# An MLA and pooling step on one core: opening, query preparation, ends of attention and small weights of the merge rearranged

## The chip, the cores and the metric
The kernel runs on one core of a Trainium2 chip. It is written engine by engine: PE (matrix products and transposes), DVE (vector), ACT (activations), POOL (GpSimd) and SP (which only issues DMAs) each have their own instruction stream, and semaphores order them. The metric is the device time of one execution in microseconds. Of three runs of the kernel before the median is 2271.24 us (2266.74 to 2272.23).

## The reference
One layer of a decoder on 2048 prompt tokens and 8 sample tokens, each of the latter with 2048 positions of paged cache. Everything is float32; in the kernel every product operand is split into a high part (rounded to the type fp32r) and a low part, the rest, and a product is made as three products (high x high, high x low, low x high).
```
h = rmsnorm(x, g_pre); z = h @ w_in       # q_lat 256, kv_lat 128, k_r 64, z_att, u_pool, z_pool, g_att, g_pool
q = (rmsnorm(q_lat, g_q) @ w_uq)          # 8 heads of 128 + 64
q_r = rope(q[128:]); q_abs = einsum(q[:128], w_uk)      # 128 a head
ckv = rmsnorm(kv_lat, g_kv); kr = rope(k_r)
s = (q_abs . ckv + q_r . kr) * SCALE, causal; o_lat = softmax(s) @ ckv
y_att = (einsum(o_lat, w_uv) * silu(z_att)) @ w_o_att
p = causal window means of u_pool (2, 4, 8, 16) - u_pool, @ w_pool, * pool_scale
y_pool = (p * silu(z_pool)) @ w_o_pool
x = x + (sigmoid(g_att) * y_att + sigmoid(g_pool) * y_pool) @ w_out;  y = rmsnorm(x, g_final)
```

## The kernel before
The work is in four stages, each a block of its own in which all engines start together: `project`, `attend`, `decode` (the sample tokens' attention) and `merge`.

`project` (names a_) takes 17 tiles of 128 rows. `steps` runs them as a pipeline: step i makes h of tile i, the latent product of tile i-1, and the queries of tile i-2 and i-3. Steps 0 to 2 are written out, the rest is a loop, and steps NT to NT+2 drain it. Two hooks stand in the written-out steps: `columns` makes the high and low part of the latent weights `wlat` (ACT L295, DVE L81 in `split`), `prepare` those of the query weights `wq`. The absorbed weights w_uq x w_uk are made by PE (L445) in PSUM; DVE multiplies them and the rotary columns with g_q (L372, L375), casts (L377) and splits. PE's latent product waits for weights_ok. SP stores h, queries, ckv and krope; the block waits for all stores at its end.

`attend` (names b_; q is read back from HBM) has 32 units, 16 query tiles x 2 groups of 4 heads. Unit u belongs to query tile u // 2, and has u // 2 + 1 key tiles. Its steps are, by kind: Q the high part of the queries (ACT L728, L729; the low part is POOL's split), S scores, five products (PE L828), C copy out of PSUM with the row maximum (DVE L778, L782), B the bias (L789), E exp (ACT L735), I the inverse of the sum, P the scaling (DVE L806), T four transposes (PE L838), H and L the high part (ACT L742) and low part (DVE L81) of the transposed weights, V three products (PE L847), O the output. The queries of a unit are five DMAs on SP (L675, L679) into one of two buffers. `attend_orders` fixes the order on PE, ACT and DVE ahead of time: a planner goes through queues of steps, by estimated durations (`takes`) and by what each step needs (`needs`). The order of the queues is the order of preference; on PE it is V, T, S. DVE's work for the sample tokens' queries (e_rows, e_q, e_qd, L757 to L763) stands ahead of its first C.

`merge` (names d_) has 5 chunks of 412 columns. ORDER lists 52 products with a weight tile each (U the pooling input, ZP, ZA, GA, GP, OA, OP, WO); their weights come through two pairs of buffers, high part on ACT (L919), low part on DVE (L81), two tiles ahead. Before the first chunk the small weights w_uv and w_pool are loaded on ACT's queue into memory that zs and u use later, and split by ACT (L1456, L1457) and DVE; DVE also makes hsum, sums of the history. POOL makes the window sums (L1579 and following), and the low part of the latent outputs, ols.


## Time and profile before
| | us |
|---|---|
| median of 3 runs | 2271.24 |
| the profiled execution | 2264.78 |
| its span, first to last instruction | 2263.0 |
| PE busy | 2150.1 (95%) |
| DVE busy | 1284.1 (57%) |
| ACT busy | 990.7 (44%) |
| POOL busy | 358.1 (16%) |
| mean granted TensorE clock | 0.984 |

The busy times are sums over the whole span, and PE is busy in nearly all of it. What PE does not fill, 113 us, is at particular places, which the timeline shows: there each row gives, in brackets, how long the engine was idle before it and which instruction released it. The idle time of the other engines costs nothing in itself. The projection goes to about 248 us, attention to 940, decode to 1006, the merge to the end.

### The profile page before, as it was taken

The page shows a single profiled execution, that of the slowest core. Times are in us where ns is not written, and L with a number is a line of the kernel's source. Part 1 is how long each engine was busy: PE and PEld are TensorE (multiplying, and loading weights), DVE is VectorE, ACT ScalarE, POOL GpSimd, SP SyncE. Part 2 cuts the span into 40 slices and gives each one's busy share as a digit, 9 for nine tenths or more (in the row PEclk, how much of TensorE's full clock was granted, in tenths as well). Part 3 has the DMA queues.
Part 4 walks back from the last instruction along what each step waited for, and adds up shares of the span by engine and source line. Part 5 has one row for each costly group of instructions (what it writes and reads, how often), then busy time and mean ns, then how long its engine had stood idle before and what let it go on. Part 6 is the DMA issues. An engine that isn't in the chain of part 4 may idle for free.

```text
span 2263.0 us, 33247 instructions
## 1 busy us (share of the span) xinstructions
PE 2150.1 (95%) x11994; PEld 1988.9 (88%) x11994; DVE 1284.1 (57%) x2632; ACT 990.7 (44%) x1774; POOL 358.1 (16%) x496
## 2 busy tenths in 40 slices
PE   4999689999999999788999999999999999999997
PEld 4888578888888888568999999999999999999997
DVE  4565377778777777335544464346544464446434
ACT  3555365555555555344333443244333433334333
POOL 1333221201100020105000420015000510032000
PEclk9999799999999999899999999999999999999999
DMA  4454332211100111244443345334534345333432
GB/s 165 152 169 152 116 89 59 53 30 33 38 24 20 29 55 63 109 140 133 149 152 121 131 135 179 117 137 130 178 119 142 114 138 171 115 122 127 175 121 69
DMA packets 132142, 252.84 MB, mean 112 GB/s; under 512 B 18394, under 2 KB 82274, under 8 KB 130710
## 3 DMA queue, kind: packets, MB, share of 16 engines
q1 hardware_dynamic: 108734, 218.17, 29.8%
q10 hardware_dynamic: 20960, 20.19, 3.1%
q0 software_dynamic: 2304, 12.58, 1.4%
q8 instruction: 88, 1.44, 0.3%
q14 instruction: 56, 0.46, 0.1%
HBM read 208.34 MB, written 42.79 MB: 111 GB/s over the span
## 4 chain that ended last, share of the span: by engine, by line
PE 52%; DVE 1%; issue 1%; ACT 0%; DVEq 0%; POOLq 0%; POOL 0%; ACTq 0%
PE d_ps L113 52%; PE d_ps L1731 1%; DVE d_gate_p L1678 0%; DVE d_mrg L81 0%; DVE d_y L1635 0%; ACT d_zs L1523 0%; ACT d_mrg L1501 0%; DVE d_ya L1682 0%; ACT d_zs L1537 0%; DVE d_y L1637 0%; DVE d_pool L81 0%; DVE d_y L1716 0%; DVE d_wr L81 0%; ACT d_wr L919 0%; POOLq L1279 0%
## 5 line engine op out<-in xcount | busy, mean ns | idle before, releaser
L113 PE MATMUL d_ps<-d_ht,d_wr 128*128 128x412 f32 x3840 | 738.3, 351 | 9.7 <-DVE d_wr L81 8.0
L113 PEld LDWEIGHTS d_ps<-d_ht,d_wr 128*128 128x128 f32 x3840 | 719.1, 188 | 14.1 <-DVE d_wr L81 8.3
L81 DVE TENSOR_TENSOR d_wr<-d_ws,d_wr 128x1024 fp32r<-128x1024 f32 x260 | 320.6, 1233 | 554.7 <-ACT d_wr L919 554.5
L919 ACT ACTIVATE d_wr<-d_ws 128x1024 fp32r<-128x1024 f32 x260 | 275.2, 1059 | 603.7 <-PE d_ps L113 601.1
L828 PE MATMUL b_ps<-kt,b_qs 128*128 128x512 f32 (+3 forms) x1600 | 359.0, 376 | 18.7 <-POOL b_qs L81 14.4
L828 PEld LDWEIGHTS b_ps<-kt,b_qs 128*128 128x128 f32 x1600 | 277.4, 194 | 65.7 <-POOL b_qs L81 15.0
L735 ACT ACTIVATE b_p<-b_p,b_bias 128x1024 f32<-128x1024 f32 (+7 forms) x192 | 172.0, 898 | 109.7 <-DVE b_low L789 106.3
L81 DVE TENSOR_TENSOR b_pt<-b_ps,b_pt 128x512 fp32r<-128x512 f32 x272 | 171.9, 683 | 81.2 <-ACT b_pt L742 80.8
L847 PE MATMUL b_ps<-b_pt,kv 128*128 128x512 f32 x816 | 209.3, 399 | 8.8 <-DVE b_pt L81 8.8
L742 ACT ACTIVATE b_pt<-b_ps 128x512 fp32r<-128x512 f32 x272 | 143.7, 596 | 143.8 <-PE b_ps L838 143.3
L847 PEld LDWEIGHTS b_ps<-b_pt,kv 128*128 128x128 f32 x816 | 151.7, 189 | 47.8 <-DVE b_pt L81 14.0
L113 PE MATMUL d_ps<-d_mrg,d_wr 128*128 128x412 f32 x960 | 190.1, 353 | 0.5
L113 PE MATMUL d_ps<-d_gat,d_wr 128*128 128x412 f32 x960 | 186.6, 350 | 0.0
L113 PEld LDWEIGHTS d_ps<-d_gat,d_wr 128*128 128x128 f32 x960 | 179.3, 188 | 0.8
L113 PEld LDWEIGHTS d_ps<-d_mrg,d_wr 128*128 128x128 f32 x960 | 176.3, 188 | 4.0 <-DVE d_mrg L81 2.2
L81 POOL TENSOR_TENSOR b_qs<-b_qf,b_qs 128x512 fp32r<-128x512 f32 x64 | 86.4, 1351 | 515.8 <-ACT b_qs L729 513.3
L782 DVE TENSOR_SCALAR_CACHE_REDUCE b_p<-b_ps 128x512 f32<-128x512 f32 x192 | 130.6, 686 | 35.7 <-PE b_ps L828 27.6
L838 PEld LDWEIGHTS b_ps<-ident,b_p 128*128 128x128 f32 x1088 | 126.0, 142 | 26.1 <-DVE b_p L806 13.8
L838 PE MATMUL b_ps<-ident,b_p 128*128 128x128 f32 x1088 | 137.6, 275 | 11.7 <-DVE b_p L806 11.5
L1579 POOL TENSOR_TENSOR d_win<-d_u 128x426 f32<-128x426 f32 x20 | 21.2, 1060 | 735.8 <-ACT d_u L1482 733.2
L806 DVE TENSOR_SCALAR b_p<-b_p,b_inverse 128x1024 f32<-128x1024 f32 (+7 forms) x192 | 124.0, 676 | 1.4
L113 PE MATMUL a_ps<-a_wlat,a_ht 128*128 128x448 f32 x408 | 89.3, 375 | 6.5 <-DVE a_wlat L81 6.5
(193 smaller groups left out, 2132.5 us busy)
## 6 DMA issues: line engine op xcount, KB each, us to landing
d_ws<-in_w SPq DMA_DIRECT2D x260, 512.0 KB, 3.5
out_q<-a_qout SPq DMA_DIRECT2D x17, 768.0 KB, 3.3
a_x<-in_x ACTq DMA_DIRECT2D x17, 512.0 KB, 3.7
out_ht<-a_hf SPq DMA_DIRECT2D x17, 512.0 KB, 4.1
d_hf<-out_ht SPq DMA_DIRECT2D x20, 412.0 KB, 3.6
d_olf<-out_olat SPq DMA_DIRECT2D x40, 206.0 KB, 3.0
b_qf<-out_q SPq DMA_DIRECT2D x32, 256.0 KB, 2.8
b_qf<-out_q SPq DMA_DIRECT2D x128, 64.0 KB, 2.6
```

The source lines that it names most:

```text
L81: return e.tensor_tensor(low, source, high.bitcast(f32), ALU.subtract)
L113: mm = pe.matmul(out, stationary(a, k), moving(b, k), start=first and k == 0 and a + b == 0, stop=last and k == depth - 1 and a == 1)
L735: act.activation(sp_[row][:, keys], sp_[row][:, keys], ACT.Exp, bias=bias[:, row:row + 1], scale=SCALE, accum_out=total[:, row, part:part ...
L742: act.activation(pt[n % NPT][:, 0, :], ps_t[n % NTB][:, :], ACT.Copy).then_inc(pt_hi, 1)
L782: dve.tensor_scalar(out, inp, 1.0, None, ALU.mult, ALU.max, accum_out=top[:, row, c:c + 1]).then_inc(s_sb, 1)
L806: dve.tensor_scalar(sp_[row][:, keys], sp_[row][:, keys], inverse[:, row:row + 1], None, ALU.mult).then_inc(p_ok, 1)
L828: mm = pe.matmul(ps_s[n % NS][:, 0:keys * P], q[:, a, h, :], kt[:, first:first + keys, b, :], start=k == 0, stop=k == len(pairs) - 1)
L838: mm = pe.transpose(ps_t[n % NTB][:, h * P:h * P + P], sp_[(u % 2) * HG + h][:, j * P:j * P + P], ident[:, :])
L847: mm = pe.matmul(ps_o[u % 2][:, :], kv[:, j, a, :], pt[n % NPT][:, b, :], start=j == 0 and k == 0, stop=j == tiles(u) - 1 and k == 2)
L919: act.activation(ahead["wr"][k % 2][:, 0, :, :], ahead["ws"][k % 4][:, :, :], ACT.Copy).then_inc(ahead["w_hi"], 1)
L1579: own(pool.tensor_tensor(out[:, start:HIST + T], source[:, start:HIST + T], source[:, start - shift:HIST + T - shift], ALU.add))
L1731: mm = pe.transpose(bank[xt_bank(n)][0:rows, s * P:s * P + P], yt[n % 2][:, s * P:s * P + rows], ident[:, :])
```

## The change
In the projection, g_pre, the small weights and all other inputs are loaded on SP, wlat in two halves with a semaphore each; ACT loads no inputs, and loads its table with a one-column activation at its start. It no longer waits for g_pre and the identity before its first square. PE starts the first latent product with the first half of the inner dimension. g_q is applied to the query latent of every tile (a scale in ACT's copies, a scalar_tensor_tensor on DVE) instead of to the weights. On ACT the first instructions were

```order
L287 DMA a_wuq_t<-in_w_uq_t 128x2048
L288 DMA a_wuk_t<-in_w_uk_t 128x1024
L289 DMA a_wq_f<-in_w_uq_rope 128x2x512
L302 ACT_TABLE_LOAD
L302 ACTIVATE a_junk,a_stat<-a_x 128x1024
L307 DMA a_x<-in_x 128x1024
L336 ACTIVATE a_hf<-a_ps 128x512 x2
L295 ACTIVATE a_wlat<-a_wlat_f 128x1792 x2
```

and are

```order
L314 ACT_TABLE_LOAD
L314 ACTIVATE a_warm<-a_half 128x1
L343 ACTIVATE a_junk,a_stat<-a_x 128x1024
L348 DMA a_x<-in_x 128x1024
L379 ACTIVATE a_hf<-a_ps 128x512 x2
L320 ACTIVATE a_wlat<-a_wlat_f 128x1792 x2
L343 ACTIVATE a_junk,a_stat<-a_x 128x1024
L348 DMA a_x<-in_x 128x1024
```

The three input loads are gone from ACT's queue, and a table load with `a_warm` stands first.

The buffers of attention's queries and their semaphores now belong to both stages; wlat_f and wuk_t lie in their memory during the projection. SP loads units 0 and 1 (k_qf_49 and k_qf_50, stores a_qout) before the last two stores of queries, in SP's rows of the projection's end:

```order
L243 DMA out_ht<-a_hf 1024x1x128
L249 DMA out_q<-a_qout 128x1536
L254 DMA out_ckv<-a_norm 128x128
L257 DMA out_krope<-a_norm 128x64
L550 DMA k_qf_49<-out_q 128x512
L554 DMA k_qf_49<-out_q 64x2x128 x4
L550 DMA k_qf_50<-out_q 128x512
L554 DMA k_qf_50<-out_q 64x2x128 x4
L249 DMA out_q<-a_qout 128x1536 x2
```

Before, no L550 or L554 stood there, and the stores followed each other. ACT and POOL make the high and low parts of these queries at the projection's end. The block does not wait for the stores; SP, ACT, POOL and DVE do so at the start of `attend`, PE does not.

In attention, the first eight units (SMALL) have their scores in memory of their own, so that C does not wait for an earlier unit's transposes. PE's preferences are T, V, S, and the last unit's scores go first once they are reached. `takes` has other durations and there are lags behind Q. The decode queries' work on DVE stands before unit 16's first C. PE began (b_qs the queries, kt the keys, b_p the weights of the softmax, b_pt these transposed)

```order
L828 MATMUL b_ps<-kt,b_qs 128x128 x40
L828 MATMUL b_ps<-kt,b_qs 128x256 x15
L838 MATMUL b_ps<-ident,b_p 128x128 x8
L828 MATMUL b_ps<-kt,b_qs 128x256 x10
L847 MATMUL b_ps<-b_pt,kv 128x512 x6
L828 MATMUL b_ps<-kt,b_qs 128x256 x15
L828 MATMUL b_ps<-kt,b_qs 128x384 x15
L838 MATMUL b_ps<-ident,b_p 128x128 x12
L828 MATMUL b_ps<-kt,b_qs 128x384 x5
L847 MATMUL b_ps<-b_pt,kv 128x512 x9
```

and begins (k_qs_51 and k_qs_52 are the two buffers of the queries)

```order
L911 MATMUL b_ps<-kt,k_qs_51 128x128 x20
L911 MATMUL b_ps<-kt,k_qs_52 128x128 x20
L911 MATMUL b_ps<-kt,k_qs_51 128x256 x20
L911 MATMUL b_ps<-kt,k_qs_52 128x256 x20
L911 MATMUL b_ps<-kt,k_qs_51 128x384 x20
L911 MATMUL b_ps<-kt,k_qs_52 128x384 x20
L911 MATMUL b_ps<-kt,k_qs_51 128x512 x20
L911 MATMUL b_ps<-kt,k_qs_52 128x512 x20
L911 MATMUL b_ps<-kt,k_qs_51 128x512 x5
L911 MATMUL b_ps<-kt,k_qs_51 128x128 x5
L911 MATMUL b_ps<-kt,k_qs_51 128x512 x5
L921 MATMUL b_ps<-ident,b_p 128x128 x4
```

The transposes (L921) and products (L930) of the first units stand behind the scores of units 0 to 8. At attention's end PE did

```order
L828 MATMUL b_ps<-kt,b_qs 128x512 x5
L847 MATMUL b_ps<-b_pt,kv 128x512 x3
L838 MATMUL b_ps<-ident,b_p 128x128 x12
L847 MATMUL b_ps<-b_pt,kv 128x512 x9
L838 MATMUL b_ps<-ident,b_p 128x128 x12
L847 MATMUL b_ps<-b_pt,kv 128x512 x9
L838 MATMUL b_ps<-ident,b_p 128x128 x12
L847 MATMUL b_ps<-b_pt,kv 128x512 x9
```

and does

```order
L911 MATMUL b_ps<-kt,k_qs_51 128x384 x5
L911 MATMUL b_ps<-kt,k_qs_52 128x512 x15
L921 MATMUL b_ps<-ident,b_p 128x128 x16
L930 MATMUL b_ps<-b_pt,kv 128x512 x3
L921 MATMUL b_ps<-ident,b_p 128x128 x8
L930 MATMUL b_ps<-b_pt,kv 128x512 x3
L921 MATMUL b_ps<-ident,b_p 128x128 x4
L930 MATMUL b_ps<-b_pt,kv 128x512 x3
L921 MATMUL b_ps<-ident,b_p 128x128 x4
```

Each tile's transposes are followed by another tile's products, and the last unit's scores stand before them.

In the merge, w_pool, w_uv and the history have memory of their own (inside mrg's), are loaded by SP behind two weight tiles, and their splitting stands behind step 1 of the first chunk. PE waits for it only before the first ZP product. Waits on const_in, y_zero and small_ok at the start of ACT are gone (y_zero is waited for before the first square), and the waits `wait_all(..., const_in, ...)` on all engines are `after(...)`, without const_in. ACT's rows at the start of the merge were

```order
L1453 DMA d_u<-in_w_pool 128x4x128
L1454 DMA d_zs<-in_w_uv 128x4x256
L1456 ACTIVATE d_wuv<-d_zs 128x1024
L1457 ACTIVATE d_wpl<-d_u 128x512
L919 ACTIVATE d_wr_9960<-d_ws_10884 128x1024
L1482 ACTIVATE d_u<-d_ps 128x412
L919 ACTIVATE d_wr_9961<-d_ws_10885 128x1024
L1482 ACTIVATE d_u<-d_ps 128x412
```

and are

```order
L1002 ACTIVATE d_wr_9945<-d_ws_10869 128x1024
L1569 ACTIVATE d_u<-d_ps 128x412
L1002 ACTIVATE d_wr_9946<-d_ws_10870 128x1024
L1543 ACTIVATE d_wuv<-d_wuv_f 128x1024
L1544 ACTIVATE d_wpl<-d_wpl_f 128x512
L1569 ACTIVATE d_u<-d_ps 128x412
L1621 ACTIVATE d_zs,d_fstat<-d_y 128x4x256
```

The copies L1456 and L1457 are L1543 and L1544 now, behind two weight tiles.

```diff
@@ project
+            for part in range(2):
+                at = slice(4 * part, 4 * part + 4)
+                sp.dma_start(wlat_f[:, at, :], io["w_lat"][:, at, :]).then_inc(wlat_in[part], 16)
...
-            steps(sp, step)
-            for s in (h_out, q_out, ckv_out, kr_out):
-                sp.wait_ge(s, 16 * NT)
+            steps(sp, step, load=load)
...
-            act.wait_ge(first_in, FIRST)
-            act.dma_start(wuq_t[:, :, :], io["w_uq_t"]).then_inc(wq_in, 16)
...
+            act.wait_ge(half_ok, 1)
+            act.activation(warm[:, :], half[:, 0:1], ACT.Square)
...
+                act.activation(wq[:, 0, :, 0:QROPE], wq_f[:, :, :], ACT.Copy).then_inc(wq_hi, 1)
+                for k in range(KQ):
+                    for a in range(2):
+                        act.wait_ge(absorbed, 2 * k + a + 1)
+                        act.activation(wq[:, 0, k, QROPE + 512 * a:QROPE + 512 * a + 512], ps[4 + 2 * a + k][:, :],
+                                       ACT.Copy).then_inc(wq_hi, 1)
...
-                    act.activation(qt[:, 0, :, :], ps_norm[:, 0:QR], ACT.Copy).then_inc(nt_hi, 1)
+                    for k in range(KQ):
+                        mm = act.activation(qt[:, 0, k, :], ps_norm[:, k * P:k * P + P], ACT.Copy, scale=gq[:, k:k + 1])
...
-                    split(dve, qt[:, 1, :, :].rearrange("p k t -> p (k t)"), ps_norm[:, 0:QR],
+                        dve.scalar_tensor_tensor(out=qt[:, 1, k, :], in0=ps_norm[:, k * P:k * P + P], scalar=gq[:, k:k + 1],
+                                                 in1=qt[:, 0, k, :].bitcast(f32), op0=ALU.mult, op1=ALU.subtract)
...
+                        pe.wait_ge(weights_ok, 1)
+                        done = KD // 2
+                        three_products(pe, ps_lat[:, 0:LAT], lambda a, k: ht[:, a, k, :],
+                                       lambda b, k: wlat[:, b, k, :], done, last=False)
+                        pe.wait_ge(weights_ok, 2)
@@ attend
-        "PE": [[("V", *t[1:]) for t in turns], list(turns), list(scores)],
+        "PE": [list(turns), [("V", *t[1:]) for t in turns], list(scores)],
...
-            if u >= 2:
+            if u >= SMALL:
                 out.append(("T", u - 2, tiles(u - 2) - 1))
...
+        if engine == "PE" and waiting[2] and waiting[2][0][1] == units - 1:
+            waiting = waiting[2:] + waiting[:2]
...
+            first = 512 * (u // 2) if u < SMALL else 0
+            return sp_[u % 2 * HG + h][:, first + keys.start:first + keys.stop]
...
+                if step == ("C", 2 * SMALL, 0, 0):
+                    decode_queries()
@@ merge
+            sp.dma_start(wpl_f[:, :, :], io["w_pool"]).then_inc(small_in, 16)
+            sp.dma_start(wuv_f[:, :, :], io["w_uv"]).then_inc(small_in, 16)
...
+                    if c == 0 and k == SMALL_STEP:
+                        small_high()
...
-                    wait_all(pool, const_in, CONSTS, (u_sb, c * NG + g + 1), *([(pl_f, c * NG + g - 1)] if g > 1 else []))
+                    after(pool, (u_sb, c * NG + g + 1), (small_ok, 3), *([(pl_f, c * NG + g - 1)] if g > 1 else []))
...
-                    if k == AT["ZP", 0]:
-                        pe.wait_ge(small_ok, 1)
+                    if c == 0 and k == AT["ZP", 0]:
+                        pe.wait_ge(small_ok, 2)
```

## Rows read from the trace of the kernel before
**Rows 1.** Windows: PE, PEld, DVE, ACT, POOL busy (instructions), PE's clock, DMA share, GB/s.
```profile
50.00:232.00 182.00, 178.05 (x978) 154.38 (x977) 109.44 (x193) 96.93 (x232) 60.02 (x140) 0.99 0.48 152
...
520.00:906.00 386.00, 384.83 (x2068) 325.67 (x2067) 296.30 (x838) 207.04 (x400) 38.43 (x30) 1.00 0.12 38
```

**Rows 2.** Timeline, opening: start, length, engine, line, operation, [idle before <-releaser].
```profile
13.95 1.28 DVE L393 SCALAR_TENSOR_TENSOR a_h<-a_x,a_stat,a_gpre 128x1024 f32<-128x1024 f32 x1 [13.95 <-POOL a_stat L254]
...
19.86 3.95 DVE L81 TENSOR_TENSOR a_wlat<-a_wlat_f,a_wlat 128x1792 fp32r<-128x1792 f32 x2
...
23.86 7.71 PE L113 MATMUL a_ps<-a_wlat,a_ht 128*128 128x448 f32 x24 [6.54 <-DVE a_wlat L81]
...
36.77 0.54 DVE L372 TENSOR_SCALAR a_wq_f<-a_wq_f,a_gq 128x512 f32<-128x512 f32 x1
...
42.81 3.36 DVE L81 TENSOR_TENSOR a_wq<-a_wq_f,a_wq 128x3072 fp32r<-128x3072 f32 x1
...
48.08 1.97 PE L487 MATMUL a_ps<-ident,a_h 128*128 128x128 f32 x8 [5.41 <-DVE a_h L393]
...
56.90 5.10 PE L113 MATMUL a_ps<-a_wlat,a_ht 128*128 128x448 f32 x24
```

**Rows 3.** DMA issues of the first 12 us: size, median us to landing.
```profile
a_gpre<-in_g_pre SPq DMA_DIRECT2D x1, 512.0 KB, 7.2
```

**Rows 4.** Timeline from the projection's end to the scores of unit 9.
```profile
246.65 0.66 PE L480 MATMUL a_ps<-ident,a_qrot 128*128 128x128 f32 x4 [1.30 <-DVE a_qrot L432]
...
252.21 2.65 SPq L679 DMA_DIRECT2D b_qf<-out_q  x4
...
256.54 0.63 ACT L728 ACTIVATE b_qs<-b_qf 128x512 fp32r<-128x512 f32 x1 [10.45 <-DMA b_qf<-out_q]
...
257.84 2.60 POOL L81 TENSOR_TENSOR b_qs<-b_qf,b_qs 128x512 fp32r<-128x512 f32 x2 [20.93 <-ACT b_qs L729]
...
260.49 3.46 PE L828 MATMUL b_ps<-kt,b_qs 128*128 128x128 f32 x15 [13.19 <-POOL b_qs L81]
...
266.84 0.50 DVE L763 COPY e_qd<-e_q 128x192 f32<-128x192 f32 x1 [4.51 <-DMA e_q<-out_q]
...
267.59 5.60 PE L828 MATMUL b_ps<-kt,b_qs 128*128 128x128 f32 x25 [3.64 <-DVE b_top L778]
...
339.39 5.80 PE L828 MATMUL b_ps<-kt,b_qs 128*128 128x512 f32 x32
```

**Rows 5.** Page, costliest groups: busy, mean ns | idle before, releaser.
```profile
L81 DVE TENSOR_TENSOR b_pt<-b_ps,b_pt 128x512 fp32r<-128x512 f32 x272 | 171.9, 683 | 81.2 <-ACT b_pt L742 80.8
...
L806 DVE TENSOR_SCALAR b_p<-b_p,b_inverse 128x1024 f32<-128x1024 f32 (+7 forms) x192 | 124.0, 676 | 1.4
```

**Rows 6.** Timeline of PE at attention's end.
```profile
913.47 2.82 PE L838 MATMUL b_ps<-ident,b_p 128*128 128x128 f32 x12 [5.34 <-DVE b_p L806]
...
918.65 1.47 PE L838 MATMUL b_ps<-ident,b_p 128*128 128x128 f32 x12
...
920.66 2.37 PE L847 MATMUL b_ps<-b_pt,kv 128*128 128x512 f32 x9 [0.54 <-DVE b_pt L81]
```

**Rows 7.** Timeline of the merge's first chunk, then the second from 1264.62.
```profile
1006.50 9.23 PE L113 MATMUL d_ps<-d_ht,d_wr 128*128 128x412 f32 x48 [1.67 <-PEq L980]
...
1017.14 1.06 ACT L1456 ACTIVATE d_wuv<-d_zs 128x1024 fp32r<-128x1024 f32 x1 [12.70 <-DMA d_zs<-in_w_uv]
...
1022.91 1.53 POOL L1579 TENSOR_TENSOR d_win<-d_u 128x426 f32<-128x426 f32 x1 [12.99 <-ACT d_u L1482]
...
1023.73 16.43 PE L113 MATMUL d_ps<-d_ht,d_wr 128*128 128x412 f32 x72 [8.01 <-DVE d_wr L81]
...
1055.46 0.83 PE L113 MATMUL d_ps<-d_ols,d_wuv 128*128 128x412 f32 x3
...
1264.62 22.75 PE L113 MATMUL d_ps<-d_ht,d_wr 128*128 128x412 f32 x120
...
1302.04 0.72 PE L113 MATMUL d_ps<-d_ols,d_wuv 128*128 128x412 f32 x3
```

More of the change, by code:

```diff
@@ L60 @@
 PART = 8
+SMALL = 8
 RUN = PAST // P
@@ L106, in wait_all, with after @@
         e.free_register(register)
+def after(e, *waits):
+    for sem, value in waits:
+        wait(e, sem, value)
 def three_products(pe, out, stationary, moving, depth, first=True, last=True):
@@ L694, in _ @@
                                  ).then_inc(dq_in, 16)
-            for u in range(2, units):
-                load_q(u)
+            for u in range(SMALL, units):
+                load(u)
             for n in range(2):
```

364 lines of the change are left out of this document (207 added, 157 removed).

## The prediction
> **What bounds the kernel now.** I read the windows by stage first, then PE's timeline at each place where PE is not busy. [rows 1] show that PE is the bound of the steady stretches: 178.05 of 182 us in the projection, 384.83 of 386 in the attention's middle. There a change off PE can give 1 or 2 per cent at most. The holes are at the joints, where PE's rows in the timeline carry an idle time and its releaser: PE starts the first latent product at 23.86 and stands 5.41 us before the transposes of tile 2's h [rows 2], it stands 13.19 and then 3.64 us at the start of attention [rows 4], 5.34 near its end [rows 6], and 8.01 in the first chunk of the merge [rows 7]. All parts of the change are at these places, so the sum is made place by place, each to a common point beyond which both kernels do the same work. It is made against the profiled execution, 2264.78 us (span 2263.0), which is 6.5 us under the median of the three runs, 2271.24.
>
> **Opening.** The first h waits for g_pre, which lands near 8.9 (7.2 us after the third issue of SP [rows 3]), and for POOL's two small steps behind ACT's square. Before, ACT waits for that landing, issues three loads and loads its table ahead of the square, and h starts at 13.95 [rows 2]. Now the square needs only x, g_pre is issued earlier, and h starts near 9.8: 4 us. The latent product then waits for the high and low part of its weights. They are copied and split in two halves; DVE's two take 3.95 us [rows 2], and the copies stand behind tile 0's transposed h on ACT. With ACT 4 us earlier and PE allowed to begin after the first half (another 2 us), it starts near 17.7 instead of 23.86. That is 6.1 us, if the weights land no later than before, and nothing new is ahead of them in SP's queue. Next, the weights of the queries. Before, DVE scales, casts and splits them in one row of work that starts with a scaling at 36.77 and ends with a split of 3072 columns, 3.36 us, at 46.17 [rows 2], 9.3 us in all. Tile 2's h stands behind it on DVE, and PE waits for that h (5.41 us). Now ACT makes the high parts in five copies, and DVE does only five splits, one of 1024 columns, for which I take a third of the 3.36 and a little more, 1.2 us, and four of 512 from PSUM at 0.683 [rows 5], 4.0 us. So DVE is free 5.4 us earlier on top of the 6.1, and h of tile 2 reaches PE near 37 instead of 48.08. PE's stop cost speed as well: its eight transposes at 48.08 took 1.97 us, where four took 0.66 at the end of the projection [rows 4], and the query product behind them was slow too; I count some 2 us for that. I put the latent product of tile 2 at 43.4 instead of 56.90 [rows 2]: **-13.5**. At the least it is the 6.1 of the weights plus 4 of the 5.3 of DVE, -10; at most the 6.1 plus all 9.3 us, -15.
> The price is in the loop: gq is applied to each tile's query latent, in two ACT copies of 128 columns for one of 256, and two DVE operations for one, some 0.3 us more on either in each of 17 tiles. PE hides it: ACT works 96.93 and DVE 109.44 of the 182 us where PE works 178.05 [rows 1], and h is ready about 2.5 us before PE takes it. Were that cover gone, 14 tiles of 0.3 us would cost 4 us.
>
> **Attention's start.** Before, the queries of unit 0 are loaded only when every store has landed; then follow SP's issues, ACT's copies (from 256.54), POOL's two splits of 2.60, and PE starts at 260.49 [rows 4]. Now units 0 and 1 are loaded near the end of the projection, ten DMAs put on SP ahead of the last two stores of queries (some 6 us of SP, since the last four of unit 0's five took 2.65 [rows 4]). These stores gain a few us of delay at most, and they do not hold PE. Their ACT and POOL work lies beside PE's last tile. PE's own last transposes end at 247.3. It can begin attention some 3 us later, at 250.9: 9.6 us earlier. Second, DVE's first copy of scores stands behind the decode queries, a copy at 266.84 that waited 4.51 us for its DMA [rows 4], and PE's 3.64 us stall stands behind that; with these moved back, the copy can start once the stores have landed, shortly before SP's first load of before, and the mask some 2.7 us later, at 254.5.
> What is late next: the new order has PE do the scores of units 0 to 8 in a row, without transposes. That takes a new pair of queries each time, and a buffer's round is load (4.7 us from SP's first issue, just before the row at 252.21, to ACT's copy at 256.54), two ACT copies (1.3, to POOL's start at 257.84) and POOL's splits (2.60) [rows 4] plus hand-overs, 9.2 us for two units. So scores 2, 4, 6 and 8 start at about 261, 270, 279.5 and 289, with PE idle half the time, and this phase ends near 293.5. Then stand 20 tiles of transposes and products of units 0 to 7. PE does one in 1.11 us, the 1.47 and 2.37 of three by [rows 6] less the overlap of their ends (22.2 for 20). DVE's part is the 20 splits L of 0.683 and some 16 us of scaling P, most of which has not been done before, and the scores' copies of the next units beside it; at DVE's pace I get 36 us, that is the common point, the scores of unit 9, at 329.6 instead of 339.39 [rows 4, 5]: **-9.8**. At PE's pace it would be 315.7, a gain of 23.7; with the wait for queries or for P's worse than I think, the gain falls to 5, the part that the first stall alone must leave.
> **The middle of attention.** PE's order now takes transposes, then products, then scores. There is nothing to win (1.17 us of 386 [rows 1]). Whether it costs is the open point. I take **-0.5**, between -4 and +4: -4 if all waits go and PE's queue runs closer, +4 if DVE falls behind in some bursts.
> **Attention's end.** The last unit's scores come first now, so that its softmax lies beside other units' products. [rows 6] show what goes: 5.34 us before the last unit's transposes, four waits of 0.54 before its products, the first of which is shown, and a longer one before the last, about 9 us together; and the twelve transposes behind the stop took 2.82 us against 1.47 in the next burst, and their products 2.81 against 2.37. In all 11 us. The new order alternates one tile's transposes with one tile's products; ends of the chain H, L, V stay: 2.5 us. **-9**, at least -6, at most -11.
>
> **Merge.** Chunk 0 of before against chunk 1 gives its loss: from PE's first product to the first value product 1055.46 - 1006.50 = 49.0, and in chunk 1 1302.04 - 1264.62 = 37.4, so 11.6 us [rows 7]. The rows show the cause: the small weights land late, ACT's copy of w_uv begins at 1017.14 after 12.70 idle, everything that splits the third weight tile is behind it, and PE stands 8.01 us. The other 3.6 us of the 11.6 are slower products behind the stop and the wait at the end of POOL's chain. Now they are behind the tile splits on ACT and DVE and PE should go through. What is late next is POOL: its windows wait for the sums of the history, these for the constants, whose loads stand on SP's queue behind two more issues now, so POOL starts at about 1021 instead of 1022.91. Its chain to the split of the first value operand, for which PE waits at 1055.46, took 32.5 us from 1022.91; I estimate that 4.8 of it were waits on ACT and DVE, which themselves waited for PE, and take 27.7. It ends at 1048.7, while PE arrives at 1055.46 - 11.6 = 1043.9. One wait less at each of some 30 steps gives back up to 2. So PE waits 3 to 5 us of the 11.6: **-8.5**, at most -11, at least -6.
> One rule of the Trainium skill speaks against this. The row first: POOL's first window operation, of 426 columns, took 1.53 us beside DVE's splits of weights [rows 7], and POOL's splits of 512 columns, with nothing on DVE, 1.30 each [rows 4]. The Trainium skill, "SBUF — State Buffer", section "Who interferes with whom", says that a VectorE instruction with two SBUF inputs and a GpSimd instruction that reads SBUF lock each other out for the whole instruction. By that rule alone, each of the six or so splits of some 1.2 us beside POOL's chain could add its whole length, 7 us, and merge would give only about 3, as in rival (d). I keep to the trace, since the 27.7 us already hold such delays.
>
> **Sum.** -13.5 - 9.8 - 0.5 - 9 - 8.5 = -41.3. Against the profiled execution 2223.5; with the 6.5 us between it and the median, about **2229 us**. Decode in between is unchanged.
>
> **Rivals.**
> (a) The scores in a row bring little: the saved start is spent waiting for queries and then for DVE, and the end gains only its 6. Then attention gives about 8 instead of 19, the merge 6, the opening 10: -24, or about 2247. For it: the phase is bound by query loads for 40 us. Against: the first 9.6 us of stall are certainly gone.
> (b) The DVE-bound stretch runs at PE's pace, since P's get done in the idle half of the scores phase. -13 more, about 2216. For it: DVE's scores copies for units 0 to 7 fill only some 16 of 43 us. Against: the order puts most P's later.
> (c) The other side: bursts of transposes and products without scores between them make DVE the bound all through the attention. A tile's L is 0.683, and P's 124.0 us over 272 tiles are 0.46 a tile [rows 5], together 1.14 against PE's 1.11; and where bursts run as at the end of before, one of three tiles takes 1.47 + 0.54 + 2.37 less the overlap of both, 4.2 us [rows 6], 1.4 each. There are some 250 tiles in the middle; a loss of 0.17 us a tile decides, for it cancels the 41 us, and at 0.2 the time is about 2280. Against: scores' copies are now made in advance, so the same DVE total lies in the same time.
> (d) The merge change does not do what it says: POOL's chain, or the third tile's split now behind small weights that land at 17 us, holds PE as before. Merge gives 2 and the time is 2236.
>
> **Chances.** The forecast 0.60 (2219 to 2238), (a) 0.18, (b) 0.10, (c) 0.05, (d) 0.07. The range is 2213 to 2248. A measurement of this kernel tells about 0.3%, 7 us, from no change. Faster holds all but (c) and a tenth of (a): 0.93; same 0.02; slower 0.05.
>
> **What would show it.** In the new profile: h of tile 0 at about 10 and the first latent product near 18 us; no idle of PE before tile 2's transposes; the first score at about 251, PE idle half the time to 293 with waits on POOL's query split, then waits on DVE; the last unit's transposes without the 5 us wait; in the merge no wait on a weight split, and 3 to 5 us before the first value product. The forecast fails if the middle stretch of attention has PE under 97% (then (c)), or if waits on POOL in the first 45 us of attention go past 25 us (then (a)).

## The result, and the profile after

| | before | after |
|---|---|---|
| median of the runs | 2270.74 us (2266.74 to 2272.23) | 2245.26 us (2244.68 to 2248.45) |
| profiled execution | 2264.78 | 2245.05 |
| its span | 2263.0 | 2243.3 |

The change makes the kernel 1.1% faster: ratio 0.9892, 95% interval 0.9879 to 0.9904, or 25.5 us of the 41.3 that were forecast. The time lies 16 us above the forecast and inside its range, 2213 to 2248, though above the 2219 to 2238 that the forecast itself stood for. In a later group of runs, beside the kernel before, the changed kernel took 2236.02 against 2263.23 us, ratio 0.9884 (0.9864 to 0.9903). From profile to profile the first pair shows 19.7 us.

The gain is read place by place, between PE's landmarks. Each kernel has two profiles, since one pair would mislead: the kernel before was profiled again as e5, the changed kernel as f1.

| PE's stretch, us | before | e5 (before) | after | f1 (after) | forecast gain | gain |
|---|---|---|---|---|---|---|
| start to latent product of tile 2 | 56.90 | 54.70 | 43.63 | 44.13 | 13.5 | 11 to 13 |
| from there to the first score | 203.59 | 203.66 | 194.77 | 193.97 | 9.6 | 9 to 10 |
| first score to unit 9's scores | 78.9 | 81.6 | 87.8 | 85.9 | 0.2 | -4 to -9 |
| unit 9's scores to attention's end | 599.1 | 599.0 | 592.1 | 592.0 | 9.5 | 7 |
| decode's first product to merge's first | 62.0 | 62.3 | 68.5 | 62.4 | 0 | -6.5 in the first pair, else 0 |
| merge, first product to first value product | 48.96 | 48.85 | 43.35 | 41.28 | 8.5 | 6 to 8 |

Opening and merge gave what was said of them, within 3 us. Behind its first score the attention gave next to nothing: what its end gained, its start lost, all or most of it. The work itself costs what it did; the page after, to be held against [rows 5]:

```profile
L82 DVE TENSOR_TENSOR b_pt<-b_ps,b_pt 128x512 fp32r<-128x512 f32 x272 | 181.9, 688 | 61.9 <-ACT b_pt L819 60.6
...
L890 DVE TENSOR_SCALAR b_p<-b_p,b_inverse 128x1024 f32<-128x1024 f32 (+7 forms) x192 | 125.0, 674 | 0.2
```

A split takes 0.688 us (before 0.683) and a scaling 0.674 (0.676), so the differences lie in waits and in PE's clock.

**Opening.** PE's and DVE's timeline after, to be held against [rows 2]:

```profile
9.38 1.94 PE L527 MATMUL a_ps<-ident,a_h 128*128 128x128 f32 x8 [9.38 <-DVE a_h L427]
...
16.02 1.46 PE L120 MATMUL a_ps<-a_wlat,a_ht 128*128 128x448 f32 x3 [4.70 <-DVE a_wlat L82]
...
29.28 2.48 DVE L82 TENSOR_TENSOR a_wq<-a_ps,a_wq 128x512 fp32r<-128x512 f32 x4
...
36.48 1.03 PE L527 MATMUL a_ps<-ident,a_h 128*128 128x128 f32 x8
...
43.63 2.65 PE L120 MATMUL a_ps<-a_wlat,a_ht 128*128 128x448 f32 x12
```

The first latent product starts at 16.02 instead of 23.86, tile 2's transposes at 36.48 without an idle time in brackets (before 48.08, after 5.41 idle), and they take 1.03 us where they took 1.97.

**Projection's end and the first score.** PE's timeline:

```profile
227.70 4.48 PE L120 MATMUL a_ps<-a_wq,a_qt 128*128 128x512 f32 x18 [0.19 <-DVE kt L82]
...
235.60 1.12 PE L520 MATMUL a_ps<-ident,a_qrot 128*128 128x128 f32 x4 [2.55 <-DVE a_qrot L466]
238.40 1.94 PE L911 MATMUL b_ps<-kt,k_qs 128*128 128x128 f32 x8 [1.68 <-PEq L130]
```

The first score follows the projection's last transposes by 1.7 us, where 13.19 us of waiting stood [rows 4]. The last transposes wait 2.55 us for DVE, against 1.30 before.

**Attention's start.** First the timeline of PE, ACT and DVE in a piece of it, then the windows of its two halves and of what follows, with columns as in [rows 1]:

```profile
304.48 2.36 PE L930 MATMUL b_ps<-b_pt,kv 128*128 128x512 f32 x9 [1.20 <-DVE b_pt L82]
...
306.68 1.47 PE L921 MATMUL b_ps<-ident,b_p 128*128 128x128 f32 x12
306.88 0.60 ACT L825 ACTIVATE b_ol<-b_ps 128x512 f32<-128x512 f32 x1 [2.20 <-PE b_ps L930]
307.50 0.37 ACTq L827 DMA_DIRECT2D out_olat<-b_ol  x1
307.97 1.57 ACT L819 ACTIVATE b_pt<-b_ps 128x512 fp32r<-128x512 f32 x3 [0.50 <-PE b_ps L921]
308.60 1.89 DVE L82 TENSOR_TENSOR b_pt<-b_ps,b_pt 128x512 fp32r<-128x512 f32 x3 [1.47 <-ACT b_pt L819]
...
309.35 2.37 PE L930 MATMUL b_ps<-b_pt,kv 128*128 128x512 f32 x9 [1.20 <-DVE b_pt L82]
```

```profile
238.40:285.20 46.80, 37.87 (x175) 33.71 (x175) 23.67 (x167) 27.20 (x80) 20.53 (x16) 0.78 0.45 123
285.20:326.20 41.00, 32.36 (x166) 26.29 (x167) 25.82 (x72) 18.30 (x34) 0.00 (x0) 0.88 0.22 60
...
326.20:918.31 592.11, 584.40 (x3164) 489.27 (x3163) 464.91 (x1318) 336.89 (x634) 68.17 (x51) 1.00 0.13 39
```

The scores in a row take 46.8 us (forecast 43). PE is busy for 38 of them, where the forecast had it idle half the time; its clock there is 0.78. That is no worse than the kernel before, whose same stretch in two pieces was

```profile
260.49:307.30 46.81, 36.05 (x177) 32.33 (x177) 28.31 (x149) 25.62 (x72) 18.26 (x14) 0.77 0.45 103
307.30:339.39 32.09, 30.00 (x164) 24.51 (x164) 27.07 (x96) 19.77 (x43) 5.24 (x4) 1.00 0.28 74
```

In 46.8 us either kernel does some 176 of PE's instructions, at about the same clock. The new order loses behind them, where 166 instructions take 41.0 us and 164 took 32.1. There PE is busy 32.4 of 41 us, but no engine is full: DVE, forecast as the bound, works 25.8 of 41. What PE waits for is a chain that goes from PE through ACT and DVE and back to PE. PE ends a unit's last product, ACT copies the unit's output (0.60 from 306.88) and issues its DMA (0.37), and only then does ACT make the high part of the transposes of the next unit, which PE has already begun at 306.68. DVE's low part follows, and PE's products start at 309.35 after 1.20 us idle.

**Attention's end.** In place of the 5.34 us stop and the 0.54 us waits of [rows 6], PE goes tile by tile, about 1.1 us each, with a wait of 0.36 among them:

```profile
903.12 0.60 PE L921 MATMUL b_ps<-ident,b_p 128*128 128x128 f32 x4
903.47 0.94 PE L930 MATMUL b_ps<-b_pt,kv 128*128 128x512 f32 x3
904.77 0.66 PE L921 MATMUL b_ps<-ident,b_p 128*128 128x128 f32 x4 [0.36 <-DVE b_pt L82]
```

**Merge.** PE, POOL and DVE in the first chunk, to be held against [rows 7]:

```profile
992.69 24.29 PE L120 MATMUL d_ps<-d_ht,d_wr 128*128 128x412 f32 x120 [1.67 <-PEq L1063]
...
1007.82 0.55 DVE L1714 TENSOR_REDUCE d_hsum<-d_hist 128x8 f32<-128x8 f32 x4
1008.55 0.89 POOL L1668 TENSOR_TENSOR d_win<-d_u 128x426 f32<-128x426 f32 x1 [12.46 <-DVE d_hsum L1714]
...
1024.90 0.19 POOL L1646 TENSOR_SCALAR d_fstat<-d_fstat 128x1 f32<-128x1 f32 x1
...
1032.80 1.23 DVE L82 TENSOR_TENSOR d_wr<-d_ws,d_wr 128x1024 fp32r<-128x1024 f32 x1 [1.24 <-ACT d_wr L1002]
1032.84 1.23 POOL L1646 TENSOR_SCALAR d_fstat<-d_fstat 28x1 f32<-28x1 f32 x1
...
1034.93 2.44 POOL L82 TENSOR_TENSOR d_ols<-d_olf,d_ols 128x412 fp32r<-128x412 f32 x2
...
1036.04 1.40 PE L120 MATMUL d_ps<-d_ols,d_wuv 128*128 128x412 f32 x3 [4.44 <-POOL d_ols L82]
1037.23 6.24 PE L120 MATMUL d_ps<-d_ht,d_wr 128*128 128x412 f32 x24
```

The 8.01 us stop is gone. POOL's chain, from its first window to the split for the first value product, runs from 1008.55 to 1036.0, 27.5 us (forecast 27.7), and PE waits 4.44 us for it, as forecast (3 to 5). Behind this stop three products take 1.40 us and 24 take 6.24, against 0.83 and, by [rows 7], 22.75 / 120 x 24 = 4.55. The stage as a whole, from merge's first product to the end of the span, went from 1256.5 us (1256.3 in e5) to 1250.6 (1248.9 in f1).

**Decode.** The first profile shows the 64 small products of the new tokens' keys in 7.83 us; before and in f1 they take 0.72 and 0.76. This is the 6.5 us of the table. PE has idle times there that nothing in the profile ends ("issue"); three of the rows:

```profile
931.67 0.26 PE L1279 MATMUL c_ps<-kt,e_qd 128*32 128x8 f32 x3 [0.53 <-issue]
...
934.52 0.28 PE L1279 MATMUL c_ps<-kt,e_qd 128*32 128x8 f32 x4 [1.19 <-issue]
935.94 0.17 PE L1279 MATMUL c_ps<-kt,e_qd 128*32 128x8 f32 x1 [1.13 <-issue]
```

### The profile page after: what moved, and what is told of

Same layout as the page of the kernel before. It is cut to its first block, busy times and chain, and to the rows that moved or that the text cites. A ratio compares the mean times of both kernels' runs of the same rounds, so it can differ in the third digit from the quotient of the medians.

```text
span 2243.3 us, 32505 instructions
## 1 busy us (share of the span) xinstructions
PE 2154.3 (96%) x11994; PEld 1989.9 (89%) x11994; DVE 1294.8 (58%) x2646; ACT 1010.7 (45%) x1797; POOL 355.6 (16%) x496
## 4 chain that ended last, share of the span: by engine, by line
PE 53%; POOL 1%; DVE 1%; issue 0%; ACT 0%; POOLq 0%; DVEq 0%; ACTq 0%
PE d_ps L120 53%; PE d_ps L1825 1%; POOL d_win L1668 1%; DVE d_y L1727 0%; DVE d_y L1745 0%; POOL d_fstat L1649 0%; POOL d_fstat L1646 0%; POOL d_t L1680 0%; ACT d_zs L1626 0%; POOL d_t L1679 0%; DVE d_y L1729 0%; POOL d_win L1673 0%; DVE d_y L1810 0%; DVE d_wuv L82 0%; POOLq L1363 0%
## 5 line engine op out<-in xcount | busy, mean ns | idle before, releaser
L911 PE MATMUL b_ps<-kt,k_qs 128*128 128x512 f32 (+3 forms) x1600 | 346.4, 374 | 10.3 <-POOL k_qs L82 6.1
L911 PEld LDWEIGHTS b_ps<-kt,k_qs 128*128 128x128 f32 x1600 | 282.2, 195 | 62.6 <-POOL k_qs L82 9.7
L930 PE MATMUL b_ps<-b_pt,kv 128*128 128x512 f32 x816 | 231.2, 414 | 7.4 <-DVE b_pt L82 7.4
L82 DVE TENSOR_TENSOR b_pt<-b_ps,b_pt 128x512 fp32r<-128x512 f32 x272 | 181.9, 688 | 61.9 <-ACT b_pt L819 60.6
L819 ACT ACTIVATE b_pt<-b_ps 128x512 fp32r<-128x512 f32 x272 | 157.0, 597 | 121.6 <-PE b_ps L930 65.8
L930 PEld LDWEIGHTS b_ps<-b_pt,kv 128*128 128x128 f32 x816 | 143.1, 190 | 32.6 <-DVE b_pt L82 9.2
L82 POOL TENSOR_TENSOR k_qs<-k_qf,k_qs 128x512 fp32r<-128x512 f32 x64 | 86.7, 1354 | 518.2 <-ACT k_qs L562 515.5
L921 PEld LDWEIGHTS b_ps<-ident,b_p 128*128 128x128 f32 x1088 | 129.3, 142 | 37.1 <-DVE b_pt L82 13.4
L921 PE MATMUL b_ps<-ident,b_p 128*128 128x128 f32 x1088 | 150.6, 276 | 9.2 <-DVE b_pt L82 8.9
```

The lines of the kernel that those rows point to most:

```text
L82: return e.tensor_tensor(low, source, high.bitcast(f32), ALU.subtract)
L819: act.activation(pt[n % NPT][:, 0, :], ps_t[n % NTB][:, :], ACT.Copy).then_inc(pt_hi, 1)
L911: mm = pe.matmul(ps_s[n % NS][:, 0:keys * P], q[:, a, h, :], kt[:, first:first + keys, b, :], start=k == 0, stop=k == len(pairs) - 1)
L921: mm = pe.transpose(ps_t[n % NTB][:, h * P:h * P + P], weights(u, h, slice(j * P, j * P + P)), ident[:, :])
L930: mm = pe.matmul(ps_o[u % 2][:, :], kv[:, j, a, :], pt[n % NPT][:, b, :], start=j == 0 and k == 0, stop=j == tiles(u) - 1 and k == 2)
```

## The experiments

Medians are in us. e1 to e4 ran in one group (the kernel before at 2271.48 beside them), e5 to e8 in a second (2264.37), f1 to f4 in a third (2263.23). The changed kernel itself ran only in a group of its own (before 2270.74) and as f1. Between groups only ratios can be compared, and small differences of ratios lie within their intervals; so the readings below rest on stretches of the profiles and on medians inside a group.

**e1, merge as before.** The merge (class Space to the end of merge) is the one of before, all else as after.

> The changed kernel with the merge stage as it was before. The changed merge runs 5.9 us shorter than the old one by the two traces (1250.6 against 1256.5 us from its first product to the end). If the edits of the merge make that, this kernel has the 8.0 us stop before the third weight tile again and takes about 2251 us (ratio 0.9915). The rival: the merge gains by what stands ahead of it (the state in which decode leaves queues and clock), then the stop is short here too and the time stays at 2245. In decode, theory A (the 7.4 us that 64 small products take in place of 0.7 come with how PE's instruction stream is laid out) expects them slow again, since PE's stream up to there is that of the changed kernel; theory B (chance of one execution) expects 0.7.

2248.54 us, ratio 0.9907 (0.9890 to 0.9925). The stop before the third weight tile is back, with 6.31 us. From merge's first product to the end the profile has 1255.8 us, against 1256.5 before, 1250.6 after and 1249.6 to 1250.8 in e2 to e4. The merge's part is worth 5 to 6 us by the profiles; the ratios, 0.9907 and 0.9892, would say 3, but their intervals overlap.

**e2, the old order.** The planner's costs, the sequence of PE's queues and the last-unit rule as before; for the rest as after.

```diff
-        "PE": [list(turns), [("V", *t[1:]) for t in turns], list(scores)],
+        "PE": [[("V", *t[1:]) for t in turns], list(turns), list(scores)],
...
-    lag = {("S", "Q"): 2.6, ("Q", "Q"): 7.0}
+    lag = {}
...
-SMALL = 8
+SMALL = 2
...
-        if engine == "PE" and waiting[2] and waiting[2][0][1] == units - 1:
+        if False:
```

> The changed kernel with attention's orders on PE, ACT and DVE exactly those of before (and score memory of two units); the early loads of queries, the late decode queries and all else stay. Theory A: the order with all scores first costs 9 us between the first score and those of unit 9 (87.8 against 78.9 us). Then this kernel takes about 75 us there (78.9 less the stop of 3.6 that the decode queries made), has the 11 us of holes at attention's end back, and takes 674 us for attention's PE work against 679.9: about 2240 us. Rival B: the start is held by the queries' chain or by the lower clock after the joint whatever the order; then that stretch stays at 87 us, the holes at the end come on top, and it is 2254 us. Decode's 64 small products: 0.7 us if their slowness comes from the layout of PE's stream in attention, 7.4 if from anything else in the change.

2241.48 us, 0.9870 (0.9854 to 0.9887). From the first score to unit 9's scores e2 takes 77.95 us, and from there to attention's end 599.8. e1, in the same group and with the new order, takes 85.8 and 592.3. So the new order costs 8 us at the start and brings 7.5 at the end, and both reach merge's first product at the same time, 989.67 in e2 and 989.75 in e1. (The ratio of after, 0.9892, would make the new order up to 5 us worse, but the intervals overlap.) In e2's first 46.81 us PE does 181 instructions at a clock of 0.74, in e1's 46.78 us 179 at 0.80; the rest takes 31.1 and 39.0 us. That shows where the forecast failed: with the old order the start would have kept its gain.

**e3, old order, last unit first.** e2 with the last-unit rule left in.

> As the kernel with the orders of before, but the last unit's scores go first once PE reaches them. If that rule alone makes the gain at attention's end, the holes of 11 us shrink to 2 or 3 and this kernel is 8 to 9 us under the one with the old orders: about 2231 us. If the gain at the end comes from the preference T, V, S (single tiles in turn) instead, the waits of 0.54 before each three tiles' products stay and it wins only the 5.3 us of the wait before the last transposes: about 2235.

2237.53 us, 0.9852 (0.9836 to 0.9868), 4 under e2. First score to unit 9: 77.9; from there to attention's end 596.7. The rule alone gives 3 us of the end; the waits of 0.54 us in each burst of three tiles stay, which the new alternation removes. One of them:

```profile
898.05 2.36 PE L930 MATMUL b_ps<-b_pt,kv 128*128 128x512 f32 x9 [0.54 <-DVE b_pt L82]
```

**e4, the output copy later.** After, but ACT's output copy of each of units 0 to 7 (O) is moved behind the first high part (H) of the next unit's burst.

```diff
+    act = orders["ACT"]
+    for u in range(SMALL):
+        step = ("O", u)
+        first = act.index(("H", u + 1, tiles(u + 1) - 1))
+        if act.index(step) < first:
+            act.remove(step)
+            act.insert(first, step)
     return orders
```

> The changed kernel, with ACT's copy of the finished output of units 0 to 7, and its DMA issue, moved behind the high parts of the next unit's transposes. Theory A: in the stretch from 285 to 317 us PE waits for a chain on ACT (output copy 0.6 and issue 0.4 ahead of the high part), 1.2 us a unit; without it each wait shrinks to about 0.2 and seven units give 6 us, some of it with a clock that stays up: about 2239 us. Theory B: DVE's scaling P of the next unit ends last there (1.1 to 1.7 us a unit), and the wait only moves in front of the transposes: 2244 to 2246.

2241.20 us, 0.9871 (0.9854 to 0.9887). The same place as above, in e4, then the windows:

```profile
297.15 1.57 ACT L826 ACTIVATE b_pt<-b_ps 128x512 fp32r<-128x512 f32 x3 [1.93 <-PE b_ps L928]
...
298.53 2.37 PE L937 MATMUL b_ps<-b_pt,kv 128*128 128x512 f32 x9 [0.54 <-DVE b_pt L82]
298.60 0.62 ACT L832 ACTIVATE b_ol<-b_ps 128x512 f32<-128x512 f32 x1
...
300.73 1.47 PE L928 MATMUL b_ps<-ident,b_p 128*128 128x128 f32 x12
```

```profile
238.16:284.00 45.84, 37.41 (x177) 33.33 (x178) 23.85 (x168) 27.21 (x80) 20.48 (x16) 0.80 0.44 123
284.00:319.00 35.00, 28.61 (x166) 23.44 (x166) 25.65 (x72) 17.00 (x34) 0.00 (x0) 1.00 0.25 70
```

Waits of 1.20 have become 0.54, a unit of three tiles takes 4.21 us instead of 4.87, and PE's clock stays at 1.00, so 166 instructions are busy for 28.6 instead of 32.4 us. The copy and its DMA issue ahead of the high part cost 5 to 6 us of this stretch (40.3 us in f1, 41.0 after, 35.0 here); the scores in a row before it are unchanged. Of this some is given back later: against e1, whose attention is that of the changed kernel, e4 takes 80.6 instead of 85.8 us to unit 9's scores and 593.9 instead of 592.3 from there, 3.6 us less in all.

**e5, before, unchanged.**

> The kernel before, unchanged, profiled once more. Its shown profile took 2264.78 us, under all its other runs (2266.7 to 2274.0), and has 64 small products of decode in 0.72 us; all five profiles of changed kernels so far have them in 7.8 to 8.0 us, whatever PE's order in attention. Theory A: the 7 us are an event that falls on most executions of either kernel, and the shown profile was one without it: this one then has 7 to 8 us there, and about 2271 us. Theory B: it belongs to the changed kernel: 0.7 us again, and about 2265.

One run, 2265.28 us. The small products took 0.72 us, as in the first profile of before. Other stretches show how far two profiles of one kernel can differ: 54.70 against 56.90 us in the opening, and 81.6 against 78.9 at attention's start, of which PE is busy 68.7 and 66.1 us, at a clock of 0.81 and 0.86. PE's idle time there is the same, 12.8 us.

**e6, history sums first.** In the merge the constants that the history sums need are loaded ahead of the small weights, and DVE makes the sums at step 0, not behind the small weights' splits at step 1.

```diff
+            sp.dma_start(head[:, :, :], io["head"]).then_inc(const_in, 16)
+            sp.dma_start(hist[:, :, :], io["hist_t"]).then_inc(const_in, 16)
             sp.dma_start(wpl_f[:, :, :], io["w_pool"]).then_inc(small_in, 16)
...
+                    if c == 0 and k == 0:
+                        history()
                     if c == 0 and k == SMALL_STEP:
                         small_low()
```

> The changed kernel; in the merge, the history and its head factors are loaded first and the history's sums made by DVE after the first weight tile, so POOL's chain no longer stands behind the small weights. Theory A (POOL's chain of 27.5 us from 1008.5 us on makes PE wait 4.44 us at the first value product): the chain starts some 4 to 5 us earlier, the wait is under 1 us, and the slower products behind it (1.6 us) go too: about 2239.5 us. Rival: POOL's chain gets longer by as much, since it lies beside more of DVE's splits: 2244 to 2246.

2230.62 us, 0.9849 (0.9836 to 0.9863); the changed kernel, in the next group, has 0.9884. From merge's first product to the end it takes 1243.9 us, against 1250.3 in e7 and 1250.2 in e8 beside it, whose merge is that of the changed kernel: 6.4 us less. POOL starts 9.57 us after merge's first product instead of 15.86, its chain is 2 us longer (29.4), and PE no longer waits for it:

```profile
984.92 24.29 PE L120 MATMUL d_ps<-d_ht,d_wr 128*128 128x412 f32 x120 [1.68 <-PEq L1063]
...
994.49 0.89 POOL L1668 TENSOR_TENSOR d_win<-d_u 128x426 f32<-128x426 f32 x1 [6.16 <-DVE d_hsum L1717]
...
1024.28 0.72 PE L120 MATMUL d_ps<-d_ols,d_wuv 128*128 128x412 f32 x3
```

The three products at the stop take 0.72 us again, not 1.40.

**e7, old start and new end.** The old order to the last scores of unit 9, the new sequence of queues behind it, last unit first.

```diff
-SMALL = 8
+SMALL = 2
...
-        "PE": [list(turns), [("V", *t[1:]) for t in turns], list(scores)],
+        "PE": [[("V", *t[1:]) for t in turns], list(turns), list(scores)],
...
+        if engine == "PE" and (not waiting[2] or waiting[2][0][1] > 9):
+            waiting = [waiting[1], waiting[0], waiting[2]]
```

> The changed kernel with PE's old preference (V, T, S, and score memory for two units) up to the scores of unit 9, and the new one (T, V, S, last unit's scores first) from there. The theory that the new rule costs at the start and gains at the end expects 77 to 78 us from first score to unit 9's scores, 592 us from there to the end, so about 670 us in all against 679.9: 2235.5 us. The rival: the two parts hang together (the gain at the end is paid for by work done ahead at the start), then it is no better than 2240.

2232.01 us, 0.9856 (0.9841 to 0.9871). First score to attention's end takes 674.3 us, against 679.7 in e6 and 680.0 in e8 beside it, so 5.5 us less, but not the 670 that the best parts of e2 and after would make: 79.8 to unit 9's scores and 594.5 from there. f2 has the same attention and takes 79.0 and 593.0, 672.0 in all, so 2 us of the miss are no more than two profiles differ. e7 keeps the planner's new costs and lags; since its start is near that of e2, it is the preference and the score memory that made the start slow.

**e8, latent product not in halves.** PE waits for both halves of the latent weights.

```diff
-                        pe.wait_ge(weights_ok, 1)
+                        pe.wait_ge(weights_ok, 2)
                         done = KD // 2
```

> The changed kernel, but PE's first latent product waits for both halves of the weights. If the half gives what the prediction said, the first product begins 2 us later (18.0 instead of 16.0 us), and so does the latent product of tile 2 (45.6 instead of 43.6). If the second half was the bound anyway, PE now stands there before the second half and tile 2's stays at 43.6.

One run, 2239.83 us. The first latent product starts at 18.06 instead of 16.02 (16.00 and 16.10 in e6 and e7), and tile 2's at 45.61 instead of 43.63 (43.45 and 44.34): the halves are worth their 2.0 us, and most or all of it is left at tile 2.

**f1, the changed kernel again.**

> The changed kernel unchanged, to put it beside the other runs of this chip. If the 6 us that its decode stage lost in the profile (the 64 small products of the lengths and keys took 7.83 us where the kernel before showed 0.72) belong to the kernel, the products take about 7.8 us again. If they belong to a chip or an execution and not to the program, as the runs with a late stage of the kernel changed suggest (0.77 to 0.96 us on another chip), they take about 0.8 us wherever the kernel before comes out near 2264 us, and the changed kernel then comes out near 2238 us there; the ratio stays 0.989 in both cases.

2236.02 us, 0.9884 (0.9864 to 0.9903). The small products take 0.76 us. So their slowness is a matter of the execution or of the group of runs, not of the program.

**f2, e6 and e7 together.**

> The changed kernel with two edits together: the attention's order of before up to unit 9's first scores and the new rule behind them, and merge's history sums ahead of the small weights. Alone they brought 6 and 7 us. They lie in stages that don't touch, so they add up: 13 us below the changed kernel, ratio 0.983 or 0.984 to the kernel before (2225 us where that takes 2264). If the two share a cover, less than 10 us.

2223.91 us (2223.45 to 2224.95), 0.9829 (0.9813 to 0.9844). That is 12.1 under f1. By the profiles e6 brought 6.4 us and e7 5.5, 11.9 together, so the two add up, as expected.

**f3, f2 with the output copy late**, as in e4, for units 0 to 8.

> f2 with ScalarE's output copy of the first units (O) behind the next unit's first high parts. In the changed kernel this move brought 4 to 7 us, since each unit of the first eight was one or two tiles and the copy stood in the way of the next high part. Here the first units' scores lie between the units, so the score matrices cover the copy: 0 to 2 us from f2. If the copy is what costs at the start whatever the order, 4 us.

2220.60 us (2219.24 to 2221.71), 0.9812 (0.9796 to 0.9827), 3.3 under f2. The five times of f3 all lie below the five of f2. Unit 9's scores come 74.8 us after the first, in f2 79.0; from there to attention's end it takes 594.6, in f2 593.0. So the copy costs in the old order too, nearly as much as in the new: 4.2 us of the start against 5.2 in e4, and 1.6 us are given back later in both. This is the fastest version, 15.4 us under the changed kernel.

**f4, the first queries late.** After, but units 0 and 1 are loaded, copied and split at the start of attention, as before.

```diff
-            steps(sp, step, load=load)
+            steps(sp, step)
...
-            for u in range(2, units):
+            for u in range(units):
                 query_low(pool, keep, u)
```

> The changed kernel with the queries of units 0 and 1 loaded, copied and split at the start of attention as before, not in the last steps of projection. If this part of the change brought what was forecast, the first score comes 9 to 10 us later than in the changed kernel, and the whole time is 7 to 9 us longer: the early units wait anyway later, so a few us come back. If ACT's and POOL's new work at the end of projection (the q products there start 12.3 us earlier but the last work of PE only 11.0) costs more than it hides, the loss is under 4 us.

2244.38 us, 0.9924 (0.9903 to 0.9945), 8.4 over f1. The first score:

```profile
234.65 0.66 PE L520 MATMUL a_ps<-ident,a_qrot 128*128 128x128 f32 x4 [1.30 <-DVE a_qrot L466]
248.17 10.03 PE L911 MATMUL b_ps<-kt,k_qs 128*128 128x128 f32 x44 [12.87 <-POOL k_qs L82]
```

It comes at 248.17 instead of 238.10, and all that follows is as long as in f1 (first score to attention's end 677.8 and 677.9). So the early queries give 10 us by the profiles and 8.4 by the medians, and in this the 1.25 us that the last transposes wait longer with them (2.55 against 1.30, this part's doing, since f4 has 1.30 back) are already counted. From tile 2's latent product to the first score f4 takes 204.3 us, before 203.6: applying g_q to every tile costs less than 1 us in the loop, as far as this stretch shows.

## Why the prediction was right, and where not

**Opening, -13.5: right,** with 13.3 measured in the first pair of profiles and 10.6 in the second. Two steps were off, in opposite directions. h came at 7.95, not 9.8, so the first product started at 16.02, not 17.7: 7.8 us earlier than before instead of 6.1. From there to tile 2's transposes (36.48) the gain was 3.8 us, where 5.4 had been put on DVE's shorter work. e8 shows the 2 us for the halves. That DVE's shorter preparation gives the rest is argued from the rows, not tried.

**Start of attention, -9.8: the step that failed.** The 9.6 us of the earlier first score were right (9 to 10 in the profiles, 8.4 by the medians of f4 and f1). The way from there to unit 9's scores, forecast at 78.7 us, took 87.8 and 85.9. "DVE-bound 36 us behind the scores" was wrong: the stretch took 41 us with DVE at 63%, and the row of scores before it took 46.8, not 42.6. Against the two profiles of before the new order costs 4 to 9 us here, and 8 inside one group (e1 against e2). Held against before, with the same 341 instructions of PE on record in both, idle time went from 12.85 to 17.6 us, and both second profiles have the same (12.8 and 17.5): so 5 us are waits. The busy time went from 66.05 to 70.23 us, but from 68.7 (e5) to 68.4 (f1) in the second pair. A cost of slower products is thus not shown for the whole stretch. e2 shows that it is the order, and e4 that 5 to 6 us of it are one ACT copy with its DMA issue, ahead of the next high part. The prediction counted each engine's work and took the fullest as the pace. In a burst of one to three tiles no engine is full, and what counts is the chain from one engine to the next and what stands in front of it in a queue; its sum was in [rows 6] already, as the 0.54 us, and O was never priced. The clock was left out as well. In the row of scores it makes no difference between the kernels (0.78 after, 0.77 and 0.67 in the two profiles of before), but behind it the kernel before had 1.00, and the changed one, stopping and going, 0.66 in the first 15 us (0.77 in f1):

```profile
285.00:300.00 15.00, 10.06 (x36) 7.52 (x36) 7.19 (x21) 5.24 (x9) 0.00 (x0) 0.66 0.33 90
```

**Middle and end, -9.5: 7 measured.** PE's stop and the bursts' waits went as said. Rival (c) did not come: DVE kept up with the tile-by-tile order, PE being busy 584.4 of 592.1 us. e3 puts 3 us of the 7 on the last unit's rule; the other 4 would then be the alternation's, which is not tried alone. The forecast's own sum for the end was a little high: its parts, 8.9 and 1.8 us of holes and slow products less the 2.5 that stay, make 8.2, not 9.

**Merge, -8.5: mechanism right, size 6 to 8.** Wait (4.44) and chain (27.5) were right. What the forecast had too small is the way to the wait: it took 37.4 us from chunk 1 for the time until PE arrives, and PE arrived after 38.9, since the first 120 products took 24.29 us where chunk 1's take 22.75. In f1, where they took 23.02 and the wait was 3.39, the term is 7.7. Missing too was the cost of the wait beside its length: the products behind it take 1.40 + 6.24 us instead of 0.83 + 4.55, 2.3 us more. They lie behind the first value product, so outside this term; the stage as a whole still gained 5.9 us (7.6 in f1). With e6 the wait goes and 5 to 6 us more come. On POOL the rows above show the exclusion: a POOL operation on 28 rows of one column takes 1.23 us, exactly as long as DVE's split beside it, where its likes take 0.19. That is what the Trainium skill says in "SBUF — State Buffer", "Who interferes with whom", of a VectorE instruction with two SBUF inputs; the trace agrees. But such meetings were in the 32.5 us of before as well. An estimate from the traces, the time of POOL's operations in the chain over their usual time at the same shape, gives 5.1 us before, 7.1 after and 5.5 in f1. So the rule added 2 us at most to the chain, and taking 27.7 from the trace was right.

**Rivals.** The time, 2245, is where (a) stood (2247), and (a) said of the start what happened: the saved time is spent again. It put the blame on waits for queries and on DVE, though, and gave the opening 10 and the merge 6. POOL's waits in the scores phase are 6 us, far under the 25 at which (a) was to hold. The forecast's own sum had 16 us more than came; that the time still fell inside the range is owed to (a), for which the range was made wide, and not to the sum. (b), the stretch at PE's pace, is what e4 comes nearer to, with 35.0 us there, of which PE is busy 28.6. (d) is out by e1 and e6.

**Decode, unchanged: right in the program.** In the first profile its 64 small products lost 7 us. Five profiles (after, e1 to e4) show 7.8 to 8.0 us, the other nine 0.7 to 1.0, among them f1, the same kernel. The chip alone does not explain it: the record gives the same chip number for e1 to e4 and for e5 to e8. No profile of before has the loss; that it fell on before's timed runs in the first groups is suggested by its ratio to the changed kernel being the same in both, by its median being 7 us longer there than in the later groups, and by its profiled execution lying 6 us under its median. It isn't shown. If it is so, the 6.5 us that the forecast added between profile and median were this loss. What makes PE's queue pause is open.

## What to carry over

In a short burst that passes from engine to engine, sum the chain and look at what stands in each queue ahead of its next link; the fullest engine does not set the pace there. An output copy and its DMA issue belong behind the first link of the next burst (worth 4 us of attention's start in the old order, 5 in the new, and 3 to 4 in the whole time). A stop of PE can cost more than its length (here 4.44 us, and 2.3 more in the products behind it): price these from the rows behind an older stop. Profile both kernels twice before a few us of one stretch are explained.

## What was not expected

- PE's 64 products of 128x8 took 0.72 us in one program's profile and 7.83 in another's, and then 0.76 in the same program in a later group of runs. Two profiles, one of each kernel, would have laid 7 us on the change that are not its own.
- POOL's shortest operation stretched from 0.19 to 1.23 us beside one DVE split, the length of that split.
- The kernel before, profiled twice, differs by 2.2 us in its opening and by 2.7 at attention's start. With one profile of each kernel, 4.2 us of slower products seemed to be the new order's; the second pair shows none.
- The order with all scores first does about as much in its first 46.8 us as the old one (175 instructions of PE against 177): its cost lies in the bursts that it leaves for later.
